# ScalarE's exponential of an attention unit is issued behind the copy of a preceding unit's transposed map

## The reference

```python
s = jnp.where(mask, jnp.einsum('bqhd,bkhd->bhqk', qi, k) * scale, NEG)
p = jax.nn.softmax(s, axis=-1)
o = jnp.einsum('bhqk,bkhd->bqhd', p, v)
```

## Time and profile before

| | |
|---|---|
| Median of 3 runs | 2898.91 us (2895.21 to 2900.93) |
| Profiled execution, its own span | 2914.3 us |
| PE busy | 2751.4 us, 94% |
| PE weight loads busy | 2329.2 us, 80% |
| VectorE busy | 1594.9 us, 55% |
| ScalarE busy | 1152.1 us, 40% |
| Mean granted PE clock | 0.970 |

### The profile page before, as it was taken

How to read it: one execution, slowest core, us unless ns; L and a number is a source line. 1 busy time by engine, 2 the same in 40 slices (tenths; PEclk the granted TensorE clock), 3 DMA queues, 4 the chain that set the end, 5 groups by cost and what they waited for, 6 DMA issues and landing times.

```text
span 2914.3 us, 39559 instructions
## 1 busy us (share of the span) xinstructions
PE 2751.4 (94%) x15260; PEld 2329.2 (80%) x15260; DVE 1594.9 (55%) x3412; ACT 1152.1 (40%) x2518; POOL 31.6 (1%) x32
## 2 busy tenths in 40 slices
PE   7999999999999999999998999999998689999998
PEld 7888889989888887877786777888775467788887
DVE  5454656555545565655578564343567844634446
ACT  3333432443323433343435453333345454432333
POOL 1000000000000000000000000000000000000000
PEclk9997999999999999999999999999998799999999
DMA  3201212212220121222321122323321001232322
GB/s 127 80 24 32 71 37 73 63 59 91 80 84 26 56 62 45 86 61 84 89 83 40 55 69 84 101 94 94 94 78 40 24 29 37 76 102 95 101 94 94
DMA packets 115260, 205.32 MB, mean 70 GB/s; under 512 B 13824, under 2 KB 23680, under 8 KB 114944
## 3 DMA queue, kind: packets, MB, share of 16 engines
q1 hardware_dynamic: 113920, 198.60, 22.6%
q10 hardware_dynamic: 1152, 4.20, 0.4%
HBM read 200.58 MB, written 2.10 MB: 70 GB/s over the span
## 4 chain that ended last, share of the span: by engine, by line
PE 79%; DVE 12%; ACT 7%; issue 2%; DMA 0%; DVEq 0%; ACTq 0%; SPq 0%
PE pp L2066 20%; PE pp L2068 19%; PE pp L2067 19%; PE pp L2138 5%; PE pp L2114 4%; PE pp L2126 2%; DVE wl L1632 2%; ACT wh L1445 1%; PE pp L2062 1%; PE pp L2063 1%; PE pp L2064 1%; ACT P L1561 1%; DVE P L1860 1%; PE pp L2086 1%; PE pp L2146 1%
## 5 line engine op out<-in xcount | busy, mean ns | idle before, releaser
L2066 PE MATMUL pp<-Hh,wh 128*128 128x512 f32 (+1 forms) x2304 | 860.4, 373 | 63.1 <-DVE wl L1632 24.4
L2068 PE MATMUL pp<-Hh,wl 128*128 128x512 f32 (+1 forms) x2304 | 797.7, 346 | 0.0
L2067 PE MATMUL pp<-Hl,wh 128*128 128x512 f32 (+1 forms) x2304 | 797.4, 346 | 0.0
L1632 DVE TENSOR_TENSOR wl<-raw,wh 128x512 fp32r<-128x512 f32 (+2 forms) x774 | 500.5, 671 | 461.9 <-ACT wh L1445 452.8
L1445 ACT ACTIVATE wh<-raw 128x512 fp32r<-128x512 f32 (+2 forms) x774 | 451.1, 605 | 344.8 <-PE pp L2068 290.1
L2066 PEld LDWEIGHTS pp<-Hh,wh 128*128 128x128 f32 x2304 | 445.0, 193 | 144.2 <-DVE wl L1632 30.6
L2067 PEld LDWEIGHTS pp<-Hl,wh 128*128 128x128 f32 x2304 | 445.5, 193 | 55.2 <-issue 7.0
L2068 PEld LDWEIGHTS pp<-Hh,wl 128*128 128x128 f32 x2304 | 443.6, 193 | 51.5
L2066 PE MATMUL pp<-Yh,wh 128*128 128x512 f32 (+1 forms) x1254 | 470.9, 376 | 3.8 <-DVE Yl L1652 2.0
L2068 PE MATMUL pp<-Yh,wl 128*128 128x512 f32 (+1 forms) x1254 | 448.6, 358 | 0.0
L2067 PE MATMUL pp<-Yl,wh 128*128 128x512 f32 (+1 forms) x1254 | 448.6, 358 | 0.0
(11 more groups left out here) (244 smaller groups left out, 2626.0 us busy)
## 6 DMA issues: line engine op xcount, KB each, us to landing
raw<-in_w SPq DMA_DIRECT2D x698, 256.0 KB, 2.6
raw<-in_w SPq DMA_DIRECT2D x36, 192.0 KB, 2.4
raw<-in_w SPq DMA_DIRECT2D x40, 128.0 KB, 2.0
out<-X SPq DMA_DIRECT2D x8, 256.0 KB, 2.0
con<-in_con ACTq DMA_DIRECT2D x1, 1576.0 KB, 11.7
X<-in_x SPq DMA_DIRECT2D x2, 528.0 KB, 5.9
X<-in_x ACTq DMA_DIRECT2D x2, 528.0 KB, 7.0
Z<-in_p ACTq DMA_DIRECT2D x2, 512.0 KB, 3.2
```

The source lines that it names most:

```text
L1632: e.tensor_tensor(part("wl", j), landing(j), part("wh", j).bitcast(F), ALU.subtract).then_inc(*dve.up("split", j))
L2066: e.matmul(it.ps, wh, xh, start=it.first, stop=False)
L2067: e.matmul(it.ps, wh, xl, start=False, stop=False)
L2068: e.matmul(it.ps, wl, xh, start=False, stop=it.end).then_inc(*pe.up())
```

## The change

The exponential becomes a step of its own, `exp`, which only ScalarE takes part in. `scores` no longer issues it, so the code that was ScalarE's `scores` is now its `exp`, unchanged. In the loop, the exponentials of the units whose scores a turn has issued are issued behind the first share of other work and behind the turn of unit n-2, ahead of the second share. In the paired attentions both exponentials of a pair move there, on even turns. The queues of PE, VectorE, SP and GpSimd are the same as before, instruction by instruction.

```diff
             do("scores", u=n, maps=maps, ext=ext, mask=u["mask"], scale=u["scale"], init=u["init"], ready=u["ready"], head=u.get("head"),
-               chosen=u.get("after"), now=now, sink=u.get("sink"))
+               chosen=u.get("after"), now=now)
+            u["maps"] = maps
             u["exp"] = ("act", "exp", n)
+
+        def exp(u):
+            do("exp", u=u["n"], maps=u["maps"], sink=u.get("sink"))
...
         for n, u in enumerate(heads + [None] * (deep + 1)):
-            if u and not paired:
-                scores(u)
-            elif u and n % 2 == 0:
-                scores(u)
-                scores(heads[n + 1])
+            new = []
+            if u:
+                new = [u] if not paired else heads[n:n + 2] if n % 2 == 0 else []
+            for v in new:
+                scores(v)
             if u:
                 if pend1 and "mix" in u:
                     pend1[-1]["exp"] = u["mix"](pend1[-1])
...
             if len(pend1) > (deep if u else 0):
                 turn(pend1[0])
                 pend2.append(pend1.pop(0))
+            for v in new:
+                exp(v)
             fill()
...
-    def scores(it):
+    def exp(it):
         for x, p in enumerate(it.maps):
             act.wait_ge("dve", "scored", it.u, x)
             e.activation(p.p, p.p, AF.Exp, bias=p.neg, scale=-1.0, accum_out=p.sum).then_inc(*act.up("exp", it.u))
```

More of the change, by code:

```diff
@@ L1605, in scalar_program @@
             "high": high, "copy_out": copy_out, "four_out": four_out, "heads out": heads_out, "two_heads": two_heads, "zgate": zgate, "gate": gate,
-            "forget exp": forget_exp, "forget ln": forget_ln, "relu2": relu2, "ple": ple, "scores": scores, "turn": turn, "turn_v": turn_v,
+            "forget exp": forget_exp, "forget ln": forget_ln, "relu2": relu2, "ple": ple, "exp": exp, "turn": turn, "turn_v": turn_v,
             "lambda": lam, "diff out": diff_out, "index": index}
```

## The result

The changed kernel takes 2868.58 us (median of 4 runs, 2864.8 to 2868.9) against 2899.92 us for the kernel before on the same chip (4 runs, 2895.21 to 2903.02). The ratio is 0.9887 with a 95% interval of [0.9868, 0.9906]: 31 us faster, where 18 were forecast. A repetition in a later set of runs, for which 2868 us within 3 were expected, gave 2871.4 us and 0.9878 [0.9848, 0.9908].

What follows compares the result with a forecast made beforehand. The prediction took PE, 94% busy, as the bound, with VectorE bounding the sparse mixer's picking stretch. Terms of 15.3 us plus 3 for the clock made 18.3 us, from 2898.91 to 2881 us, range 2860 to 2895.

Steps and rivals of the forecast that it cites:

- rival B: PE keeps its full clock where short gaps now take it down: 2850 to 2870 us; chance 0.13.
- sparse mixer: picking, tail, second attention: Second block: 2.6 us of VectorE's waits for splits, 2.5 of PE's for the copy, 2.7 and 1.2 in the second attention.
- differential, first window, dilated, first of all: Four other attentions: PE's waits for late copies and splits shrink, 1.3 + 1.2, 1.5, 1.1 and 1.2 us.
- The remaining attentions keep PE full: 0: All attentions not priced singly: PE is over 90% busy there, so nothing is gained, 0 us.
- clock: The 25 us at half clock from 220 to 245 may regain full clock: 3 us, between 0 and 12.5.
- the example at 215: First attention: a split behind the exponential delays VectorE 0.73 us, then PE 0.93 and 0.85; 1.2 us taken in all.
- half of 5.2: Picking stretch of the sparse mixer: VectorE's 5.2 us wait for splits falls to about half, gaining 2.6 us.
- in the picking stretch PE's wait for the copy cannot be won: Up to 2345 VectorE bounds, so PE's 22.4 us can't be won; the whole-span wait falls from 30.0 to under 18.
- under other names: Picking stretch: PE's waits reappear at the exponential or VectorE's scores, with VectorE's busy time unchanged.
- The wait of 5.93 us behind the head copies: Sparse mixer at 2328.35: PE's wait stays, since the head copies wait for VectorE's rotation and the copy follows them.
- A: Only ScalarE's copies gain, splits move little: 6.5 us at best, 2892 to 2896 us; chance 0.17.
- C: Differential attention: VectorE's mix waits for later exponentials, up to 2 us a unit, 30 us, net 2914; chance 0.05.

Runs made afterwards that it cites:

- the first profile: Profiled execution of the kernel before, no edit, on which the prediction was based: span 2914.3 us, mean clock 0.970.
- the second set of runs: Later set in which the changed kernel was repeated (6 runs) in turns with the kernel before: 2871.4 us, ratio 0.9878.
- the second profile of the change: Another profiled execution of the changed kernel, no edit; it agrees with the other one within 0.3 us in each of eleven attention stretches.
- the second-share version: Changed kernel with the exponential behind the second share of filling work too, in all attentions: 2857.95 us, ratio 0.9834; repeated 2857.24 us, 0.9839.
- the next-turn version: Changed kernel with the exponential a whole loop turn later, in the differential attention only behind the second share: 2855.3 us, ratio 0.9833.
- the version ahead of the copy: Changed kernel with the exponential behind the first share of filling work but still ahead of the copy of unit n-2: 2878.27 us, ratio 0.9911.

## Why the prediction was right, and where it was off

**Right: what is won and that the side is faster.** The order of ScalarE's queue was the cause, and the total lies in the range of 2860 to 2895, though 12 us below the forecast and below its own range (2870 to 2890). 2868.58 us is a time that the prediction gave to rival B, the clock (2850 to 2870), and the gain is not B's: the eleven stretches are 32.4 us shorter, and their length times (1 − clock) is 24 us before and 25 after. That the range reached down to 2860 was owed to B, so that the total lies inside is in part luck. Beside its terms, by the stretches:

| step of the prediction | forecast | measured |
|---|---|---|
| sparse mixer: picking, tail, second attention | 2.6 + 2.5 + 3.9 = 9.0 | 4.9 + 2.8 + 5.9 = 13.6 |
| differential, first window, dilated, first of all | 2.5 + 1.5 + 1.1 + 1.2 = 6.3 | 2.8 + 2.3 + 1.8 + 1.9 = 8.8 |
| "The remaining attentions keep PE full: 0" | 0 | 10.0 (8.6 against the first profile, 8.5 at full clock by itself) |
| sum | 15.3 | 32.4 |
| the rest of the program | not priced | −4.6 |
| clock | 3 | about 5 in the second set of runs |

**The step that failed** is "The remaining attentions keep PE full: 0". Over 90% busy is not full: PE was idle for 3 to 4 us in the low-rank attentions and in the second forget-gate attention. I had taken the gaps from L2126 alone, the transposes that wait for a copy, and from the example at 215. The same view had more rows: whole span, PE's waits at the small piece (its transpose L2121, 3.1 us, and its scores L2111, 2.8 us, both for VectorE's copy out of bank 5) and at the scores (L2114, 2.9 us). They are now 0.8, 0.9 and 1.8 us, 5.3 us less together. The row for the weights (L2066, 25.6 us before, 23.0 after) is no part of it: it lies almost wholly outside the attentions, and the second profile of the change has 25.5. In each of these rows VectorE is late; its wait for splits fell in the same attentions, by 5.7 to 7.0 us each, and the splits had stood behind an exponential. The lateness that the prediction followed for L1874 has the same effect on whatever VectorE does next.

The example of the earlier trace rows was read half right. The gap of 0.93 us closed to 0.11. The one of 0.85 us, which waits for the gating of an output, did not come from the split; it is the same after:

```profile
211.40 0.40 PE L2117 MATMUL pp<-K,Q 66*128 66x16 f32 x2 [0.85 <-DVE tmp L1901]
```

**Sizes.** For the other two groups the terms were 1.5 and 1.4 times too small. Taking half of each of VectorE's waits is one reason. It is not the only one: the second attention of the mixer and the tail gained more than all their listed waits (5.9 against 5.2 us, 2.8 against 2.5). In the second, 4.4 us of the 5.9 are PE's idle time, and the other 1.5 us stay open. In the picking stretch the guess "half of 5.2" for VectorE's wait was 3.6 us in the event (5.2 to 1.6), and the stretch is 4.9 us shorter. The gain of the differential attention does not last: some 36 us behind its end, at the start of the dilated one, the change is where the kernel before was (116.9 and 116.5 us from the start of the differential stretch, at a clock of 0.96 and 0.99, which is some 3.5 us). What was won there went to the clock.

**The argument that held best** is that in the picking stretch PE's wait for the copy cannot be won. Forecast was a fall of that wait from 30.0 to under 18 us, with the remainder ahead of 2345: it is 16.1, and 15.9 of it lies there. The tail and the second attention lost theirs entirely. That it could not be won also shows in the kind of what is left: in the picking stretch the change takes away 7.1 us of that wait (23.0 to 15.9 between the same matmuls), PE gets a new one of 4.4 us for VectorE's division, as the prediction had it ("under other names"), and the stretch gets shorter with VectorE's idle time (12.6 to 8.2 us between the same matmuls). The wait of 5.93 us behind the head copies was forecast to stay; it is there, and it is longer, since PE arrives at it with fewer waits behind it. The timeline after, at that place (start, length, what, idle before and its releaser):

```profile
2292.58 0.62 ACT L1529 ACTIVATE M<-tmp 32x512 f32<-32x512 f32 x1
...
2293.23 0.38 ACT L1578 ACTIVATE PT<-pp 128x256 f32<-128x256 f32 x1
...
2293.64 0.61 ACT L1567 ACTIVATE P<-P,st 128x384 f32<-128x384 f32 x1
...
2293.76 0.66 PE L2132 MATMUL pp<-con,P 128*128 128x128 f32 x2 [9.72 <-ACT PT L1578]
```

ScalarE goes from the last head copy straight to the copy of the map, and only then to the exponential: the new order, with the old wait of the head copies for VectorE still ahead of it.

**The clock.** The term was 3 of a possible 12.5 us, for the stretch at half clock. Its price was near (11.8 us), its reason was wrong, since an execution of the unchanged kernel had the full clock there. What remains is a difference of means: in the second set of runs, before took 2905.2 us on the average and the change 2870.7, 34.5 us less, of which 29.4 at full clock and 5.1 by the clock; the scatter of before's clock alone (0.967 to 0.978) is larger than that. The Trainium skill (TensorE: Matmul & The Clock Gate, Part 1) has it that activity releases the throttle, which made rival B. For the change no run shows it beyond the scatter. For the two versions that go further the runs point the same way: (1 − clock) × time is 76.7 us on the average of the 40 runs of before, 72.0 for the ten of the change, 63.2 for the ten of the second-share version and 57.8 for the four of the next-turn version. Some 14 to 23 us of it lie in the picking stretch in every version, where they cost next to nothing. And the version ahead of the copy has 64.4 with more waits than the change, so no run isolates the rule.

**The rivals.** A (only the copies gain, 6.5 us at best) fell with the version ahead of the copy: the part it denies is worth 19 to 25 us. C (the mix late) did not come. In the differential attention VectorE's wait for splits went down (3.3 to 0.4 us), no wait of the mix for an exponential appears, and PE has one of 0.5 us for the mix:

```profile
PE pp L2132 <- DVE M L1921: 0.5, 1, 0.5
```

The second-share version delays the exponential further without bringing it on. C's arithmetic was right that this attention has the least room: moving VectorE's step by the same amount cost 12 us there.

**What stays open.** Which gaps set the clock: it is better in the versions that leave PE the fewest gaps, but the version ahead of the copy, with 13.7 us more of waits for the copy, also has 0.9776. The rest of the program takes 4.6 us more with the change, some 4 us of it by the lower clock in these two profiles; why is open. And some 3 us of the forget-gate attention's gain are busy time of PE, of which the clock explains 1.7; ends of matmuls are modelled in the profile, so I make nothing of it. That the splits' earlier end also brought fetches forward was not tested by itself.

## What to carry to other kernels

An instruction at the head of an in-order queue that waits while nobody needs its result early should stand behind the work of later due time that is ready: here the exponential, which waited 370 us, moved behind a split and a copy for 30 us, and behind all of the turn's other work for 44 us. What tells which instruction may move is what its *operand* holds up: the exponential's map had two loop turns to spare, VectorE's masking, at the head of the same chain, lost 12 us by the same move. In pricing such a move, take all waits of the bound engine for the engines downstream of the queue, however short and under whatever line; "over 90% busy" left 8.5 us in the four attentions that I had put at nothing. And a step that gains must be looked at beyond its own stretch, and in the bounding engine's terms: of PE's wait of 30 us for the copy some 23 us stood in a stretch that was VectorE's.

## What the runs showed of the hardware that I had not expected

The same program ran at a mean granted clock of 0.967 to 0.978 from one execution to the next, which moved its time by 28.6 us, as much as the change. Time multiplied by clock stayed within 6 us over those 40 runs. The lower clock costs time only where PE is what the time hangs on: the same 102 matmuls took 24.93 us at 0.50 and 13.16 at 1.00, but in the picking stretch, which is VectorE's, 3.8 us more of it made 0.3 us. So the product compares runs of one version, and misleads by up to 7 us between versions. A stretch at half clock in one profile (25 us at 220 to 245) was at 1.00 in the next profile of the same kernel.
